# The values' products ahead of queries and keys in two attention layers

## The chip, the cores and the metric

The kernel runs on one core of a Trainium2 chip. The metric is the device time of one execution in microseconds (us). The core has five engines with instruction streams of their own: TensorE (PE, matrix products; PEld is its loading of stationary operands), VectorE (DVE), ScalarE (ACT), GpSimd (POOL) and SyncE (SP, which starts the DMA transfers). They wait for each other through semaphores. TensorE writes to PSUM, a memory of eight banks with 512 float32 values per partition each.

## The reference, cut to what matters

The whole program is a block with two feed-forward parts and an mLSTM mixer on 272 tokens, followed by a second block with two attention layers on 256 tokens and 1024 channels. The change is in the first step of these two layers:

```python
for l in range(DEPTH_2):                                   # two layers
    shift, scale, gate = jnp.split(c_act @ w_ada[l] + b_ada[l], 3, axis=-1)
    h = rms_norm(x, pre_norm_g[l]) * (1.0 + scale[:, None, :]) + shift[:, None, :]
    proj = h @ w_in[l]                                     # 256 x 1024 times 1024 x 4096
    q, k, v = proj[..., 0:A], proj[..., A:2*A], proj[..., 2*A:3*A]   # A = 512 columns each
    ...                                                    # gates and convolution from the rest
    att = dilated_attention(q, k, v, rel_bias) * jax.nn.silu(g_att)
    x = x + gate[:, None, :] * rms_norm(jnp.concatenate([att, cnv], axis=-1) @ w_out[l], post_norm_g[l])
```

## The kernel before

**Products.** Each float32 operand is held as a sum of two float32r parts: the weights as `w1` + `w2`, the layer's input as `u1` + `u2`. A product takes three matmuls: `w1`·`u1`, `w2`·`u1`, `w1`·`u2`. The input is stored with channels on the partitions, in eight tiles (`kt` = 0 to 7) of 128 channels by 256 tokens.

**Weights.** They arrive in chunks of 128 x 1024 values, by one fixed list, in the order of use. SP loads chunk `c` into `raw`, ACT casts it to `w1` (line 738), DVE subtracts to make `w2` (line 1032). There are five slots each. The cast of a chunk waits until TensorE has finished with the chunk five places ahead (`last_of`). The last four casts that ACT makes ahead of a layer are those of the layer's first four chunks; the fifth stands behind the input tiles in ACT's program.

**Boundary into a layer.** Between the previous stage's last product and the layer's first, the kernel normalises. TensorE turns the two scales of the norm into full tiles with transposes (line 373, `spread`): the first, `r1`, goes to PSUM bank 6, the second, `r2`, to bank 5. Then, in steps `k` = 0 to 7, DVE multiplies the previous stage's result by bank 6 (line 1223, `yg`), DVE or POOL adds it to the residual `hT`, DVE multiplies by bank 5 (line 1263, `tmp`), ACT makes `u1` (line 842) and DVE makes `u2` (line 1244). Only the last of the eight readings of a bank raises the bank's semaphore:

```python
m = e.scalar_tensor_tensor(tmp[:, k % 4, 0:n], hT[:, k, OFF[s]:OFF[s] + n], gain(k), ps[:, 5, 0:n],
                           ALU.mult, ALU.mult)
if k == KT - 1:
    m.then_inc(*reading(("r2", s)))
else:
    m.then_inc(*tick(s_tmp, (s, k)))
```

Meanwhile TensorE runs products of a dummy tile `dz` into bank 4 (`dense`, line 329) so that it doesn't stand idle.

**Banks.** `place` gives a block of products its bank: one of banks 0 to 3 in turn, or a bank named by the caller, and it makes TensorE wait until every earlier reading of that bank is done:

```python
if uses[b]:
    e.wait_ge(s_bank[b].handle, uses[b])
```

**The layer before the change.** `head` starts four of the eight query and key blocks together (banks 0 to 3): six `dense` products, then tile by tile eight matmuls with `u1[kt]` (lines 354, 355) and four with `u2[kt]` (line 358). `block` then does one block at a time, 24 matmuls of 256 columns (lines 313 to 315). Behind the eight blocks stand the values: two accumulations of 512 columns in banks 5 and 6, chunk by chunk, 48 matmuls in all (recorded on line 665). Scores (line 629) and twenty more blocks follow. Order on every engine is as the program is written.

Of the kernel before, what the change touches and what calls it, by code (L numbers as in the profile page):

```python
# [13 lines left out]
P = 128  # L14
D = 1024
KT = D // P
S = 256
# [66 lines left out]
def tick(signal, event):  # L84

    signal.count += 1
    signal.at[event] = signal.count
    return signal.handle, 1
# [13 lines left out]
def build(nc, xT, wst, wada, vec, cst, tab, rb, outT):  # L102
    ctx = ExitStack()
    with ctx:
# [184 lines left out]
        def reading(key):  # L289

            return s_bank[bank[key][0]].handle, 1
# [4 lines left out]
        def tensor(e):  # L296
# [20 lines left out]
            def block(key, c, x1, x2, n, mid=None, where=KT - 2):  # L317
                e.wait_ge(s_split.handle, c + 1)
                b = place(key)
                for kt in range(KT):  # L320
                    if mid and kt == where:
                        mid()
                    m = products(ps[:, b, 0:n], c, kt, x1[:, kt, :], x2[:, kt, :], kt == 0, kt == KT - 1)
                m.then_inc(*tick(s_proj, key))
                last_of[c] = key
# [51 lines left out]
            def u_of(s):  # L377
                return (lambda k: (s_u1.handle, at(s_u1, (s, k)))), (lambda k: (s_u2.handle, at(s_u2, (s, k))))
# [240 lines left out]
            def attention(l):  # L619
                x1, x2 = u1[:, :, 0:S], u2[:, :, 0:S]  # L620
                c = C_L[l]

                def scores(k):
                    e.wait_ge(*read(("qk", l, 4 + k)))
                    b_ = [place(("s", l, 2 * k + i), 4 + 3 * i) for i in range(2)]
                    for t in range(2):
                        for i in range(2):
                            hp = 64 * i
                            m = e.matmul(ps[:, b_[i], S * t:S * t + S], qk[l][hp:hp + 64, k, 128 * t:128 * t + 128],  # L629
                                         qk[l][hp:hp + 64, 4 + k, :], start=True, stop=True)  # L630
                    m.then_inc(*tick(s_score, (l, k)))

                def transposes(h):
                    e.wait_ge(s_nrm.handle, at(s_nrm, (l, h, 1)))
                    b = place(("pt", l, h), 5)
                    for j in range(2):
                        for t in range(2):
                            m = e.transpose(ps[:, b, S * j + 128 * t:S * j + 128 * t + 128],  # L638
                                            Sb[l][:, h % 4, t, 128 * j:128 * j + 128], ident)
                    m.then_inc(*tick(s_ptr, (l, h)))  # L640

                def values(k):
                    e.wait_ge(*read(("pt", l, 2 * k + 1)))
                    b = place(("o", l, k), 6)
                    for j in range(2):
                        for i in range(2):
                            h, hp = 2 * k + i, 64 * i
                            m = e.matmul(ps[hp:hp + 64, b, 0:S], Vt[l][:, j, 64 * h:64 * h + 64], PT[l][:, i, j, :],  # L648
                                         start=j == 0, stop=j == 1, skip_group_check=True)
                    m.then_inc(*tick(s_val, (l, k)))  # L650

                keys = [("qk", l, j) for j in range(8)]
                head(keys[:4], c, x1, x2, S, *u_of(f"l{l}"))
                for j in range(4, 8):
                    block(keys[j], c + j, x1, x2, S)
                b_ = [place(("V", l, tt), 5 + tt) for tt in range(2)]
                for c4 in range(4):
                    cc = c + 8 + c4
                    e.wait_ge(s_split.handle, cc + 1)
                    for kk in range(2):  # L660
                        kt = 2 * c4 + kk
                        a, bw = w1[:, cc % NW, 512 * kk:512 * kk + 512], w2[:, cc % NW, 512 * kk:512 * kk + 512]
                        for tt in range(2):
                            for i, (xx, ww) in enumerate(((x1, a), (x1, bw), (x2, a))):
                                m = e.matmul(ps[:, b_[tt], :], xx[:, kt, 128 * tt:128 * tt + 128], ww,  # L665
                                             start=kt == 0 and i == 0, stop=kt == 7 and i == 2)
                    m.then_inc(*tick(s_proj, ("V", l, c4)))
                    last_of[cc] = ("V", l, c4)
                for i in range(21):
                    k, p_ = i // 4, i % 4  # L670
                    if p_ in (0, 1) and 0 < k < 5:
                        transposes(2 * k - 2 + p_)
                    if p_ == 0 and k < 4:
                        scores(k)
                    if p_ == 3 and 0 < k:
                        values(k - 1)
                    if i < 20:
                        block(("g", l, i), c + 12 + i, x1, x2, S)
# [48 lines left out]
        def scalar(e):  # L727
# [12 lines left out]
            def proj(key):  # L740
                e.wait_ge(s_proj.handle, at(s_proj, key))
# [185 lines left out]
            def attention(l):  # L927
                c = C_L[l]

                def tanh_of(key, before):  # L930
                    proj(key)
                    if before:
                        e.wait_ge(*read(before))
                    e.activation(cw_[l][:, 4, :], out_of(key), ACT.Tanh, scale=0.5).then_inc(*tick(s_tanh, key))

                def split_mix(k, src):
                    e.copy(m1[l][:, k, :], src).then_inc(*tick(s_m1, (l, k)))

                split_to(c + NW - 1)
                for j in range(8):  # L940
                    if j > 3:
                        split_to(c + j + NW - 1)
                    proj(("qk", l, j))
                    b = bank_of(("qk", l, j))
                    e.copy(qk[l][:, j, :], ps[:, b, S - 1::-1] if j < 4 else ps[:, b, 0:S]).then_inc(*reading(("qk", l, j)))
                split_to(c + 11 + NW - 1)
                proj(("V", l, 3))
                for tt in range(2):
                    e.copy(Vt[l][:, tt, :], ps[:, 5 + tt, :]).then_inc(*reading(("V", l, tt)))

                def transposes(h):
                    e.wait_ge(s_ptr.handle, at(s_ptr, (l, h)))
                    if h > 1:
                        e.wait_ge(s_val.handle, at(s_val, (l, h // 2 - 1)))
                    e.copy(PT[l][:, h % 2, :, :], ps[:, 5, :].rearrange("p (j q) -> p j q", q=S)).then_inc(
                        *reading(("pt", l, h)))

                def scores(k):
                    for i in range(2):
                        h = 2 * k + i  # L960
                        e.wait_ge(s_max.handle, at(s_max, (l, h)))
                        for t in range(2):
                            e.activation(Sb[l][:, h % 4, t, :], Sb[l][:, h % 4, t, :], ACT.Exp, bias=st_[l][:, h % 4, t:t + 1],
                                         accum_out=st_[l][:, h % 4, 2 + t:3 + t]).then_inc(*tick(s_exp, (l, h, t)))

                before = None
                for i in range(21):
                    k, p_ = i // 4, i % 4
                    if p_ in (0, 1) and 0 < k < 5:
                        transposes(2 * k - 2 + p_)  # L970
                    if p_ == 0 and k < 4:
                        scores(k)
                    if p_ == 3 and 0 < k:
                        e.wait_ge(*read(("o", l, k - 1)))
                        split_mix(k - 1, at_[l][:, (k - 1) % 2, :])
                    if p_ == 0 and k > 1:
                        e.wait_ge(s_cp.handle, at(s_cp, (l, k - 2)))
                        split_mix(4 + k - 2, cw_[l][:, 2, :])
                    if i == 20:
                        break  # L980
                    key = ("g", l, i)
                    split_to(c + 12 + i + NW - 1)
                    if i < 4 or p_ == 3:
                        tanh_of(key, before)
                        before = key
                    elif p_ == 0:
                        proj(key)
                        if k > 1:
                            e.wait_ge(*read(("g", l, i - 3)))
                        e.copy(cw_[l][:, 0, :], out_of(key)).then_inc(*reading(key))  # L990
# [821 lines left out]
```

## Time and profile before

| | before |
|---|---|
| median of 3 runs | 806.5 us (806.33 to 807.24) |
| the profiled execution | 806.2 us, of which 804.2 us is the span of the profile |
| TensorE busy | 795.3 us (99%) |
| VectorE busy | 594.5 us (74%) |
| ScalarE busy | 416.5 us (52%) |
| GpSimd busy | 143.6 us (18%) |
| granted TensorE clock, mean | 0.992 of full speed |

The span is the time from the first to the last recorded instruction, 2.0 us less than the execution's time. Shares of busy time are averages over the span. Matmul records overlap: a record lasts from issue to the last result, so a stream of them is read from the starts. "Granted clock" is 1.00 at 2.4 GHz and 0.50 at 1.2 GHz. The rows that matter are listed further down.

### The profile page before, as it was taken

What the parts mean: (1) busy time and instruction counts of PE and PEld (TensorE: products, weight loads), DVE (VectorE), ACT (ScalarE), POOL (GpSimd) and SP (SyncE); (2) the same over time, 40 slices, a digit from 0 to 9 for tenths busy, and PEclk for the clock granted to TensorE, in tenths of its full rate; (3) what the DMA queues carried; (4) which work ended last, traced back from release to release, by engine and by line L of the source; (5) the groups of instructions that cost most, each with busy time, mean ns of one, the idle gap of its engine ahead of it and who ended that gap; (6) DMA issues with size and microseconds to landing.
All of it is one profiled execution on the core that took longest, in us unless ns stands there. A gap on an engine that the chain in (4) does not pass through costs nothing.

```text
span 804.2 us, 15615 instructions
## 1 busy us (share of the span) xinstructions
PE 795.3 (99%) x6338; PEld 771.1 (96%) x6338; DVE 594.5 (74%) x952; ACT 416.5 (52%) x710; POOL 143.6 (18%) x159
## 2 busy tenths in 40 slices
PE   9999999999999999999999999999999999999997
PEld 9999999999999999999999999999899999999986
DVE  6877777698786976778777779996667568567753
ACT  7444444454367565565444445536555454555541
POOL 3800000041320000020000004230245302035510
PEclk9999999999899999999999999999999999999999
DMA  9876777695436632559867679546544651744531
GB/s 342 308 250 226 233 247 249 204 325 178 122 112 215 192 130 81 182 175 298 287 218 266 241 239 339 177 145 211 163 151 129 185 161 53 264 154 133 157 106 52
DMA packets 45190, 158.83 MB, mean 197 GB/s; under 512 B 5040, under 2 KB 6576, under 8 KB 45120
## 3 DMA queue, kind: packets, MB, share of 16 engines
q1 hardware_dynamic: 45120, 157.85, 59.1%
q8 instruction: 50, 0.82, 0.4%
q14 instruction: 20, 0.16, 0.1%
HBM read 156.76 MB, written 1.06 MB: 196 GB/s over the span
## 4 chain that ended last, share of the span: by engine, by line
PE 97%; issue 1%; DVE 1%; POOL 0%; ACT 0%; DVEq 0%; POOLq 0%
PE ps L313 26%; PE ps L315 25%; PE ps L314 25%; PE ps L665 3%; PE ps L354 2%; PE ps L358 2%; PE ps L355 2%; PE ps L366 2%; PE ps L329 1%; PE ps L557 1%; PE ps L629 1%; PE ps L648 1%; PE ps L638 1%; PE ps L691 1%; PE ps L689 1%
## 5 line engine op out<-in xcount | busy, mean ns | idle before, releaser
L1032 DVE TENSOR_TENSOR w<-raw,w 128x1024 fp32r<-128x1024 f32 x245 | 300.0, 1238 | 132.6 <-ACT w L738 132.2
L313 PE MATMUL ps<-u,w 128*128 128x256 f32 (+1 forms) x1231 | 353.2, 287 | 0.0
L315 PE MATMUL ps<-u,w 128*128 128x256 f32 (+1 forms) x1231 | 349.6, 284 | 0.0
L314 PE MATMUL ps<-u,w 128*128 128x256 f32 (+1 forms) x1231 | 349.0, 284 | 0.0
L738 ACT CAST w<-raw 128x1024 fp32r<-128x1024 f32 x245 | 254.0, 1049 | 122.4 <-PE ps L315 102.7
L313 PEld LDWEIGHTS ps<-u,w 128*128 128x128 f32 x1231 | 232.0, 188 | 6.2 <-issue 4.3
L315 PEld LDWEIGHTS ps<-u,w 128*128 128x128 f32 x1231 | 232.3, 189 | 0.0
L314 PEld LDWEIGHTS ps<-u,w 128*128 128x128 f32 x1231 | 231.7, 188 | 0.0
L313 PE MATMUL ps<-h,w 128*128 128x272 f32 (+1 forms) x352 | 99.7, 283 | 0.0
L314 PE MATMUL ps<-h,w 128*128 128x272 f32 (+1 forms) x352 | 99.3, 282 | 0.0
L315 PE MATMUL ps<-h,w 128*128 128x272 f32 (+1 forms) x352 | 99.1, 282 | 0.0
L1582 POOL TENSOR_TENSOR sqa<-sqa,sq 128x272 f32<-128x272 f32 (+1 forms) x12 | 14.1, 1175 | 311.0 <-ACT sq L803 311.0
L313 PEld LDWEIGHTS ps<-h,w 128*128 128x128 f32 x352 | 66.2, 188 | 0.0
L314 PEld LDWEIGHTS ps<-h,w 128*128 128x128 f32 x352 | 66.1, 188 | 0.0
L315 PEld LDWEIGHTS ps<-h,w 128*128 128x128 f32 x352 | 66.1, 188 | 0.0
L1616 POOL TENSOR_SCALAR Sb<-Sb,st 128x256 f32<-128x256 f32 x32 | 45.2, 1428 | 87.7 <-DVE st L1460 87.7
L1051 DVE SCALAR_TENSOR_TENSOR acc<-adr,cact,acc 128x1024 f32<-128x1024 f32 x42 | 57.3, 1383 | 0.4 <-DMA adr<-wada 0.4
L781 ACT ACTIVATE si<-tmp 128x272 f32<-128x272 f32 (+1 forms) x44 | 18.7, 425 | 70.4 <-DVE tmp L1144 70.4
L1149 DVE TENSOR_TENSOR hf<-si,ps 128x272 f32<-128x272 f32 (+1 forms) x44 | 18.9, 430 | 21.1 <-ACT si L781 21.1
L1593 POOL TENSOR_TENSOR rst<-sst,eps 128x2 f32<-128x2 f32 (+1 forms) x4 | 3.0, 748 | 149.7 <-DVE sst L1195 135.1
L354 PE MATMUL ps<-u,w 128*128 128x256 f32 (+1 forms) x105 | 28.2, 297 | 1.0 <-ACT u L842 0.7
L355 PE MATMUL ps<-u,w 128*128 128x256 f32 (+1 forms) x105 | 27.6, 293 | 0.0
(246 smaller groups left out, 1043.1 us busy)
## 6 DMA issues: line engine op xcount, KB each, us to landing
raw<-wst SPq DMA_DIRECT2D x245, 512.0 KB, 4.6
adr<-wada SPq DMA_DIRECT2D x48, 512.0 KB, 4.0
Bt<-bias_rows SPq DMA_DIRECT2D x8, 192.0 KB, 3.9
hT<-xT SPq DMA_DIRECT2D x4, 272.0 KB, 4.5
outT<-yg SPq DMA_DIRECT2D x4, 256.0 KB, 2.0
cs<-cst SPq DMA_DIRECT2D x1, 140.0 KB, 5.3
cs<-cst SPq DMA_DIRECT2D x1, 128.0 KB, 6.5
vc<-vec SPq DMA_DIRECT2D x1, 101.0 KB, 3.7
```

What stands on the lines that cost most here:

```text
L313: e.matmul(out, a, x1, start=first, stop=False)
L314: e.matmul(out, a, x2, start=False, stop=False)
L315: return e.matmul(out, b, x1, start=False, stop=last)
L354: e.matmul(ps[:, b, 0:n], w1[:, (c + j) % NW, o:o + P], x1[:, kt, :], start=i == 0, stop=False)
L355: e.matmul(ps[:, b, 0:n], w2[:, (c + j) % NW, o:o + P], x1[:, kt, :], start=False, stop=False)
L665: m = e.matmul(ps[:, b_[tt], :], xx[:, kt, 128 * tt:128 * tt + 128], ww, start=kt == 0 and i == 0, stop=kt == 7 and i == 2)
L738: e.copy(w1[:, k % NW, :], raw[:, k % NRAW, :]).then_inc(*tick(s_upper, k))
L781: e.activation(si[f][:, j % 2, :], zg[:, j % 2, 0:n], ACT.Silu).then_inc(*tick(s_si, (f, j)))
L1032: e.tensor_tensor(w2[:, k % NW, :], raw[:, k % NRAW, :], w1[:, k % NW, :].bitcast(F32), ALU.subtract).then_inc(*tick(s_split, k))
L1051: e.scalar_tensor_tensor(a, w, x, a, ALU.mult, ALU.add).then_inc(*tick(s_acc, k))
L1149: e.tensor_tensor(hf[f][:, i, :], si[f][:, i, :], out_of(ku, n), ALU.mult).then_inc(*reading(ku))
L1616: e.tensor_scalar(Sb[l][:, h % 4, t, :], Sb[l][:, h % 4, t, :], st_[l][:, h % 4, 4 + t:5 + t], None, ALU.mult).then_inc(*tick(s_nrm, (l, h ...
```

## The change

In each attention layer TensorE no longer begins with `head`. It places the two accumulations of the values (banks 5 and 6), runs the six `dense` products, and takes the input tile by tile for the values: four matmuls of 512 columns with `u1[kt]`, two with `u2[kt]`. All eight query and key blocks follow with `block`. The weights' chunks are reordered to match, and so is ACT's program. DVE, POOL and SP keep their programs. The number of matmuls and their shapes stay the same.

```diff
-                keys = [("qk", l, j) for j in range(8)]
-                head(keys[:4], c, x1, x2, S, *u_of(f"l{l}"))
-                for j in range(4, 8):
-                    block(keys[j], c + j, x1, x2, S)
-                b_ = [place(("V", l, tt), 5 + tt) for tt in range(2)]
-                for c4 in range(4):
-                    cc = c + 8 + c4
...
+                b_ = [place(("V", l, t), 5 + t) for t in range(2)]
+                high, low = u_of(f"l{l}")
+                dense(6)
+                for kt in range(KT):
+                    cc, o = c + kt // 2, 512 * (kt % 2)
                     e.wait_ge(s_split.handle, cc + 1)
...
+                    a, bw = w1[:, cc % NW, o:o + 512], w2[:, cc % NW, o:o + 512]
+                    e.wait_ge(*high(kt))
+                    for t in range(2):
+                        e.matmul(ps[:, b_[t], :], x1[:, kt, 128 * t:128 * t + 128], a, start=kt == 0, stop=False)
+                        e.matmul(ps[:, b_[t], :], x1[:, kt, 128 * t:128 * t + 128], bw, start=False, stop=False)
+                    e.wait_ge(*low(kt))
+                    for t in range(2):
+                        m = e.matmul(ps[:, b_[t], :], x2[:, kt, 128 * t:128 * t + 128], a, start=False, stop=kt == KT - 1)
+                    if kt % 2:
+                        m.then_inc(*tick(s_proj, ("V", l, kt // 2)))
+                        last_of[cc] = ("V", l, kt // 2)
+                for j in range(8):
+                    block(("qk", l, j), c + 4 + j, x1, x2, S)
...
-                split_to(c + NW - 1)
+                split_to(c + 3 + NW - 1)
+                proj(("V", l, 3))
+                for tt in range(2):
+                    e.copy(Vt[l][:, tt, :], ps[:, 5 + tt, :]).then_inc(*reading(("V", l, tt)))
                 for j in range(8):
-                    if j > 3:
-                        split_to(c + j + NW - 1)
+                    split_to(c + 4 + j + NW - 1)
...
-                split_to(c + 11 + NW - 1)
-                proj(("V", l, 3))
-                for tt in range(2):
-                    e.copy(Vt[l][:, tt, :], ps[:, 5 + tt, :]).then_inc(*reading(("V", l, tt)))
...
+        parts.append(w[:, 1024:1536].reshape(4, 2, P, 512).transpose(0, 2, 1, 3).reshape(4, P, CH))
         parts.append(cols(w[:, 0:1024]))
-        parts.append(w[:, 1024:1536].reshape(4, 2, P, 512).transpose(0, 2, 1, 3).reshape(4, P, CH))
```

TensorE at the boundary into layer 0, before the change, from the fill between the two spreads to the first tile's products (`ps<-cs,rst` is a spread, `ps<-dz` a fill product, `bank5_read` the count of readings of bank 5, `u1_made` that of ready tiles):

```order
L329 MATMUL ps<-dz 128x256 x6
L373 MATMUL ps<-cs,rst 128x128 [waits bank5_read,pow_made]
L373 MATMUL ps<-cs,rst 128x128
L329 MATMUL ps<-dz 128x256 [waits bank2_read,bank1_read,bank3_read,bank0_read,w2_made]
L329 MATMUL ps<-dz 128x256 x5
L354 MATMUL ps<-u,w 128x256 [waits u1_made]
```

The same place with the change:

```order
L329 MATMUL ps<-dz 128x256 x6
L373 MATMUL ps<-cs,rst 128x128 [waits bank5_read,pow_made]
L373 MATMUL ps<-cs,rst 128x128
L329 MATMUL ps<-dz 128x256 [waits bank6_read,bank5_read]
L329 MATMUL ps<-dz 128x256 x5
L661 MATMUL ps<-w,u 128x512 [waits u1_made,w2_made]
L662 MATMUL ps<-w,u 128x512
L661 MATMUL ps<-w,u 128x512
L662 MATMUL ps<-w,u 128x512
L665 MATMUL ps<-w,u 128x512 [waits u2_made]
```

The first fill product behind the second spread waited for readings of banks 0 to 3 and now waits for those of banks 5 and 6; the products behind the fill are of 512 columns.

ACT behind the input tiles of layer 0, before the change (`u<-tmp,mod` is `u1`, `w<-raw` a chunk's cast, `qk<-ps` a block's copy out of PSUM):

```order
L842 ACTIVATE u<-tmp,mod 128x256 [waits tmp_made] x7
L842 ACTIVATE u<-tmp,mod 128x256 [waits bank5_read]
L738 CAST w<-raw 128x1024 [waits proj_done,raw_landed4]
L945 COPY qk<-ps 128x256 [waits proj_done] x4
L738 CAST w<-raw 128x1024 [waits proj_done,raw_landed0]
L738 CAST w<-raw 128x1024 [waits proj_done,raw_landed1]
L738 CAST w<-raw 128x1024 [waits proj_done,raw_landed2]
L738 CAST w<-raw 128x1024 [waits proj_done,raw_landed3]
```

And with the change:

```order
L740 CAST w<-raw 128x1024 [waits proj_done,raw_landed4]
L740 CAST w<-raw 128x1024 [waits proj_done,raw_landed0]
L740 CAST w<-raw 128x1024 [waits proj_done,raw_landed1]
L740 CAST w<-raw 128x1024 [waits proj_done,raw_landed2]
L944 COPY Vt<-ps 128x512 [waits proj_done]
L944 COPY Vt<-ps 128x512
L740 CAST w<-raw 128x1024 [waits proj_done,raw_landed3]
L949 COPY qk<-ps 128x256 [waits proj_done]
```

Four casts stand ahead of the first copy out of PSUM where one stood, and the values' copies come first.

## Rows read from the trace of the kernel before

**Rows 1.** The page: span, busy time of each engine, chain that ended last.

```profile
span 804.2 us, 15615 instructions
PE 795.3 (99%) x6338; PEld 771.1 (96%) x6338; DVE 594.5 (74%) x952; ACT 416.5 (52%) x710; POOL 143.6 (18%) x159
...
PE 97%; issue 1%; DVE 1%; POOL 0%; ACT 0%; DVEq 0%; POOLq 0%
```

**Rows 2.** Timeline of PE, boundary into layer 0: start, length, line, operation, idle before.

```profile
534.25 0.43 PE L373 MATMUL ps<-cs,rst 128*128 128x128 f32 x2 [0.45 <-POOL rst L1598]
534.49 0.95 PE L329 MATMUL ps<-dz 128*128 128x256 f32 x6
535.79 0.39 PE L354 MATMUL ps<-u,w 128*128 128x256 f32 x1 [0.35 <-ACT u L842]
...
537.33 0.28 PE L354 MATMUL ps<-u,w 128*128 128x256 f32 x1
...
538.75 0.28 PE L354 MATMUL ps<-u,w 128*128 128x256 f32 x1
```

**Rows 3.** Timeline of DVE and ACT there: last readings of banks 6 and 5.

```profile
535.45 0.47 DVE L1263 SCALAR_TENSOR_TENSOR tmp<-hT,G,ps 128x256 f32<-128x256 f32 x1
...
542.40 0.41 DVE L1223 TENSOR_TENSOR yg<-yg,ps 128x256 f32<-128x256 f32 x1
...
543.83 0.47 DVE L1263 SCALAR_TENSOR_TENSOR tmp<-hT,G,ps 128x256 f32<-128x256 f32 x1
...
535.96 0.51 ACT L842 ACTIVATE u<-tmp,mod 128x256 fp32r<-128x256 f32 x1 [0.21 <-DVE tmp L1263]
```

**Rows 4.** The same boundary into layer 1, PE and DVE.

```profile
669.56 0.43 PE L373 MATMUL ps<-cs,rst 128*128 128x128 f32 x2 [0.27 <-POOL rst L1598]
671.11 0.39 PE L354 MATMUL ps<-u,w 128*128 128x256 f32 x1 [0.38 <-ACT u L842]
...
679.16 0.47 DVE L1263 SCALAR_TENSOR_TENSOR tmp<-hT,G,ps 128x256 f32<-128x256 f32 x1
```

**Rows 5.** Timeline of PE: sixth query and key block, values, scores (layer 0); values, scores (layer 1).

```profile
550.15 0.39 PE L313 MATMUL ps<-u,w 128*128 128x256 f32 x1
...
558.78 11.29 PE L665 MATMUL ps<-w,u 128*128 128x512 f32 x48
570.00 1.14 PE L629 MATMUL ps<-qk 64*128 64x256 f32 x8
...
694.08 11.29 PE L665 MATMUL ps<-w,u 128*128 128x512 f32 x48
705.30 1.13 PE L629 MATMUL ps<-qk 64*128 64x256 f32 x8
```

**Rows 6.** Timeline of PE, boundary out of the first feed-forward part.

```profile
215.20 0.90 PE L373 MATMUL ps<-cs,rst 128*128 128x128 f32 x3 [0.50 <-POOL rst L1598]
216.03 1.65 PE L329 MATMUL ps<-dz 128*128 128x256 f32 x6
217.48 0.43 PE L354 MATMUL ps<-u,w 128*128 128x272 f32 x1
...
219.52 0.43 PE L354 MATMUL ps<-u,w 128*128 128x272 f32 x1
...
221.52 0.29 PE L354 MATMUL ps<-u,w 128*128 128x272 f32 x1
...
222.66 0.28 PE L354 MATMUL ps<-u,w 128*128 128x272 f32 x1
```

**Rows 7.** Busy time by half microseconds: PE, PEld, DVE, ACT, POOL, granted clock, DMA.

```profile
221.00:221.50 0.50, 0.50 (x4) 0.50 (x3) 0.50 (x3) 0.30 (x1) 0.00 (x0) 0.53 0.00 0
...
340.50:341.00 0.50, 0.50 (x5) 0.38 (x4) 0.38 (x2) 0.00 (x0) 0.46 (x1) 0.93 0.00 0
341.00:341.50 0.50, 0.50 (x4) 0.48 (x3) 0.00 (x0) 0.00 (x0) 0.00 (x0) 0.50 0.00 0
...
344.00:344.50 0.50, 0.50 (x5) 0.50 (x4) 0.50 (x3) 0.00 (x0) 0.28 (x1) 0.65 0.86 352
```

**Rows 8.** Waits of PEld in layer 0, 536 to 666 us: total, times, longest.

```profile
PEld ps L313 <- DVE w L1032: 0.7, 2, 0.4
```

**Rows 9.** The page's costliest groups: casts and subtractions of the chunks.

```profile
L1032 DVE TENSOR_TENSOR w<-raw,w 128x1024 fp32r<-128x1024 f32 x245 | 300.0, 1238 | 132.6 <-ACT w L738 132.2
...
L738 ACT CAST w<-raw 128x1024 fp32r<-128x1024 f32 x245 | 254.0, 1049 | 122.4 <-PE ps L315 102.7
```

More of the change, by code:

```diff
@@ L650, in values @@
                     m.then_inc(*tick(s_val, (l, k)))
-                keys = [("qk", l, j) for j in range(8)]
-                head(keys[:4], c, x1, x2, S, *u_of(f"l{l}"))
-                for j in range(4, 8):
-                    block(keys[j], c + j, x1, x2, S)
-                b_ = [place(("V", l, tt), 5 + tt) for tt in range(2)]
-                for c4 in range(4):
-                    cc = c + 8 + c4
-                    e.wait_ge(s_split.handle, cc + 1)
-                    for kk in range(2):
-                        kt = 2 * c4 + kk
-                        a, bw = w1[:, cc % NW, 512 * kk:512 * kk + 512], w2[:, cc % NW, 512 * kk:512 * kk + 512]
-                        for tt in range(2):
[L664 to L668, printed above, removed]
+                b_ = [place(("V", l, t), 5 + t) for t in range(2)]
[3 more added lines that the diff above has]
+                    cc, o = c + kt // 2, 512 * (kt % 2)
+                    e.wait_ge(s_split.handle, cc + 1)
+                    a, bw = w1[:, cc % NW, o:o + 512], w2[:, cc % NW, o:o + 512]
[11 more added lines that the diff above has]
+                    block(("qk", l, j), c + 4 + j, x1, x2, S)
                 for i in range(21):
@@ L946, in attention @@
                 split_to(c + 11 + NW - 1)
-                proj(("V", l, 3))
-                for tt in range(2):
-                    e.copy(Vt[l][:, tt, :], ps[:, 5 + tt, :]).then_inc(*reading(("V", l, tt)))
                 def transposes(h):
```

## The prediction

> **What bounds the kernel now.** I first read the page's busy times and chain: TensorE is busy for 795.3 of 804.2 us and makes up 97% of the chain that ended last [rows 1]. So a microsecond in which TensorE stands still is a microsecond of the result, and nothing that only relieves VectorE or ScalarE shows. Then I read TensorE's timeline at the boundary into layer 0, the place where the new order begins. The second spread starts at 534.25, six fill products at 534.49, and the first tile's products of the four query and key blocks at 535.79, after 0.35 us of idle time that ended with the first `u1` tile [rows 2]. The head's steps then start at 537.33 and 538.75 [rows 2], 1.42 us each; eight of them keep TensorE busy while VectorE is still normalising. That cover is what the change must keep. Third I read who uses banks 5 and 6 in that time. VectorE reads bank 6 for the last time from 542.40 to 542.81, and bank 5 from 543.83 to 544.30 [rows 3]. Fourth, for the price of a stop, I looked at the two other boundaries of the kernel, where the granted clock is at half [rows 6, 7].
>
> **The change, part by part.** *The new wait.* The values' accumulations are placed in banks 5 and 6, and these hold the two scales from which VectorE is making the very input tiles that the values' products want. Only the eighth reading raises a bank's semaphore. The first fill product behind the second spread now waits for both banks, and TensorE works in order, so behind it stand the other five fill products, all products of values, queries and keys, and everything later. Bank 5 comes last. VectorE's normalisation waits for nothing of TensorE's behind the second spread, so it runs as before and reaches its last reading at 544.30. A consumer starts about 0.05 us after such a step: a `tmp` ends at 535.92 and ScalarE takes it at 535.96 [rows 3]. So the fill starts at 544.35 instead of 534.49. TensorE's last work ahead of it, the spread, ends at 534.68 [rows 2], which leaves 9.67 us without an instruction. All of it lay under TensorE's work before: the head covered it.
>
> *The fill.* Six fill products take 1.45 us from their first start to the next instruction's where the clock is at half (216.03 to 217.48 [rows 6]). At full clock the last of six ends 0.95 us after the first start [rows 2]; a record of 0.28 us leaves 0.67 for five steps, 0.13 each, so a next instruction would start after about 0.8 us. What the clock is after this stop I take from the nearest rows: at the boundary out of the first feed-forward part 0.50 us of idle time ahead of 215.20 among short instructions went with products at half speed [rows 6], and at the one out of the mixer the clock fell to 0.50 without any stop, at about 340.93 (a mean of 0.93 over the half microsecond puts 0.07 us of it at half) [rows 7]. A stop of 9.67 us, almost twenty times the longest of these, can hardly leave it at full. I take 1.45, and the values start at 544.35 + 1.45 = 545.80. Their place in the sequence was 535.79: a shift of 10.0 us (9.35 at full clock, 544.35 + 0.79 - 535.79). Layer 1 repeats it: the last reading of bank 5 ends at 679.63, the values start at 679.68 + 1.45 = 681.13, and the head started at 671.11 [rows 4]: 10.0 us.
>
> *The rest of the half clock.* No 512-column product at half clock is in the trace. The nearest rows are the 272-column products of the first boundary: nine of them take 2.04 us (217.48 to 219.52) at half and 1.14 us (221.52 to 222.66) at full clock [rows 6], 0.227 and 0.127 us each. In proportion to the columns a values' product takes 0.427 us at half clock; at full clock 48 take 11.22 us (558.78 to 570.00), 0.234 us each [rows 5]. So a stretch at half clock loses 1 - 0.234/0.427 = 45% of itself. How long it lasts behind the resumption has two bounds: from 215.20 to the return at about 221.47 (a mean of 0.53) it is 6.25 us, from 340.93 to the return at about 344.35 it is 3.4 us (0.65 as the mean of the last half microsecond) [rows 6, 7]. Less the 1.45 us of fill already counted, 1.95 to 4.8 us lose 0.9 to 2.2 us; I take the middle, 1.5, since the two rows are equally near. The Trainium skill (TensorE: Matmul & The Clock Gate, What's actually happening) says that an idle TensorE drops to 1.2 GHz and has to be busy for a while before it gets 2.4 GHz back, which speaks against this change in the same way. The same page (Wait — 56ns, not 53.3ns?) gives 426.7 and 215.7 ns between 512-column products at the two clocks; by these the stretch would lose 49% and my middle would be 1.7 instead of 1.5 us. The trace's 234 ns at full clock is above the page's 215.7, and no row here shows the 426.7.
>
> *The moved products.* Before, the head and four blocks took 558.78 - 535.79 = 22.99 us. Now eight blocks stand there. Three took 558.78 - 550.15 = 8.63 us [rows 5], 2.88 each, so eight take 23.0. The values' 48 products are the same in either place (11.22 us in both layers [rows 5]). By the time that they start, all input tiles are made or within 1 us of it, so their tile-by-tile waits find nothing to wait for. I cost this at 0.
>
> *The weights.* The values need chunks `c` to `c+3`, which are cast ahead of the normalisation as the head's four were. The next cast, of `c+4`, stands behind the tiles on ScalarE as before and is long done when the first query block wants it, now some 21 us later. Slots then come free one every 2.8 us instead of four together, and a cast (1.05 us) and a subtraction (1.24 us) per slot fit in [rows 9]. Before, weights that VectorE had not yet made cost TensorE 0.7 us in a layer [rows 8]. That is the most this part can give; part of it was hidden under queued products, so I take 0 and keep -0.7 for the range. SP's program is the same list of loads with other addresses; it is ahead by five chunks at the stop and so gains nothing that TensorE could use. ScalarE's two copies of the values (banks 5 and 6 again) move from behind the last chunk of values to before the query blocks; the next user of either bank comes twelve blocks behind the values.
>
> *Sum.* A layer: 10.0 + 1.5 + 0 + 0 = 11.5 us. Two layers: 23.0. On the profiled execution's 806.2 us (804.2 span, 2.0 around it) that is 829.2 us; the median of the runs shown, 806.5, is 0.3 above that execution, and I add that. I predict 829.5.
>
> **The rivals.** *The stop without the clock.* The wait is as above but the clock is at full when work resumes: 9.35 a layer, 18.7 together, 824.9 us. For it speaks only that the boundaries into the two layers are the ones that kept full clock so far, with fill products in between; against it that those fills are what now waits. 4%.
>
> *The stop is partly given back.* The same stop, but ready weights and tiles behind it save TensorE's little waits: 0.7 us a layer, so 1.4 off whatever else holds, 827.9 us with the clock's price. Against it: TensorE is the bound in the whole rest of the program, and the other engines can run no more than five chunks ahead. 8%.
>
> *No stop at all, the other side.* The values start with the first tile. That needs bank 5 free of its last reading by about 535.2, when the fill would be over, and not at 544.30. Then a tile's step is six products of 0.234, 1.40 us, against 1.42 in the head, 0.2 us less in eight steps, and with the 0.7 us of weights' waits gone the layer would win 0.9, the kernel 1.8: 804.4 us. The point from which it decides is a wait of 0.9 us: if the last reading came later than that behind the fill, the change loses. Such a start would mean that the wait in the order shown is met by an earlier reading than the eighth; the program's count of readings gives bank 5 one reading for the whole scale, the eighth, which speaks against it. 3%, with a case in which stop and gain cancel within noise inside it at 1%.
>
> **How the numbers follow.** The likeliest, stop and half clock without giving back, has 85%, and its own range is that of the half clock: 806.2 + 2 x (10.0 + 0.9) = 828.0 to 806.2 + 2 x (10.0 + 2.2) = 830.6. To hold eight in ten with the unknown parts, the range reaches down towards the stop without the clock (824.9) and up to 831.5, since a stop much longer than any in the trace may keep the clock at half somewhat longer than 6.25 us. What this kernel's measurement can tell from no change is about 0.2%, 1.6 us. All cases with the stop are slower by over 2%: 97%. Faster has 2%, within 0.2% has 1%.
>
> **What would show it.** Right: in the changed kernel's timeline TensorE has one idle stretch of about 9.7 us in front of the first fill product at each of the two boundaries, released by VectorE's `tmp` step; granted clock 0.50 from there until 2 to 5 us into the values' products; the values' records longer there; TensorE's busy share falls from 99 to about 97%; no other group of waits grows. The eight blocks behind take 23.0 us. Wrong: if the idle stretch is released by anything else, if it is shorter than 9 us, or if the clock stays at 1.00, the size is off; if the first product of values starts within a microsecond of the first `u1` tile, the whole argument is.

## The result and the profile after

The changed kernel takes 827.77 us (median of 4 runs, 826.95 to 828.75); the kernel before took 806.55 us in 4 runs beside it. The ratio is 1.026 with a 95% interval of 1.0247 to 1.0273: slower by 21.2 us. The profiled execution took 828.75 us, with a span of 826.8, so it is 22.55 us above the profiled execution of before and a microsecond above its own median. Its terms are read against the profile of before, the comparison of kernels against the medians.

The page of the changed kernel: span, busy times, and the chain that ended last by engine; these answer to [rows 1].

```profile
span 826.8 us, 15633 instructions
PE 799.4 (97%) x6338; PEld 774.6 (94%) x6338; DVE 595.5 (72%) x952; ACT 416.5 (50%) x710; POOL 144.0 (17%) x159
...
PE 94%; DVE 4%; issue 1%; ACT 0%; POOL 0%; DVEq 0%; POOLq 0%
```

TensorE's busy time grew by 4.1 us with the same 6338 matmuls, and VectorE has 4% of the chain where it had 1%. The waits of TensorE in the changed kernel, total, times, longest, say where:

```profile
PE ps L329 <- DVE tmp L1264: 19.2, 2, 9.6
```

The timeline of TensorE at the boundary into layer 0, answering to [rows 2], and into layer 1, answering to [rows 4]: start, length, line, operation, idle before.

```profile
533.95 0.43 PE L373 MATMUL ps<-cs,rst 128*128 128x128 f32 x2 [0.47 <-POOL rst L1599]
544.00 1.65 PE L329 MATMUL ps<-dz 128*128 128x256 f32 x6 [9.62 <-DVE tmp L1264]
545.45 0.63 PE L661 MATMUL ps<-w,u 128*128 128x512 f32 x1
545.87 0.63 PE L662 MATMUL ps<-w,u 128*128 128x512 f32 x1
...
557.94 0.28 PE L313 MATMUL ps<-u,w 128*128 128x256 f32 x1
...
580.72 1.13 PE L629 MATMUL ps<-qk 64*128 64x256 f32 x8
...
681.07 0.63 PE L373 MATMUL ps<-cs,rst 128*128 128x128 f32 x2
691.30 1.65 PE L329 MATMUL ps<-dz 128*128 128x256 f32 x6 [9.61 <-DVE tmp L1264]
692.75 0.63 PE L661 MATMUL ps<-w,u 128*128 128x512 f32 x1
...
705.04 0.28 PE L313 MATMUL ps<-u,w 128*128 128x256 f32 x1
...
727.82 1.14 PE L629 MATMUL ps<-qk 64*128 64x256 f32 x8
```

VectorE's timeline there, answering to [rows 3]: the last reading of bank 5.

```profile
543.47 0.47 DVE L1264 SCALAR_TENSOR_TENSOR tmp<-hT,G,ps 128x256 f32<-128x256 f32 x1
```

It ends at 543.94 and the fill starts at 544.00 ("the resumption" from here on: the first product behind the stop). By then all input tiles but the last `u1` and the last two `u2` are made; the values' products come when nothing is left to cover. A useful measure of a layer is the time from the start of the second spread to the start of the scores, since everything that moved lies between them: before, 35.75 us (534.25 to 570.00) and 35.74 (669.56 to 705.30) [rows 2, 4, 5]; now 46.77 and 46.75. That is 22.0 of the 22.6 us by which the span grew. The rest lies between the layers: from the first scores to layer 1's second spread it is 99.56 us before and 100.35 now, less 0.3 us by which layer 0's second spread came earlier. The clock was at half there from 678.2 to 681.6 in this execution. The profiles of the kernels below have 99.5 to 99.6 us in the same place where the clock stayed at full, and 100.05 and 100.06 us in the two others where it was at half, so the order isn't the cause.

Busy time and granted clock (the number behind the five engines) of the changed kernel, early and late in the stop and where full speed came back in layer 0, then early in the stop and where full speed came back in layer 1:

```profile
534.50:536.00 1.50, 0.00 (x0) 0.00 (x0) 1.50 (x4) 0.85 (x2) 1.23 (x2) 0.62 0.04 14
...
540.00:544.00 4.00, 0.01 (x1) 0.01 (x1) 4.00 (x10) 1.55 (x4) 1.88 (x3) 0.50 0.00 0
...
548.00:548.50 0.50, 0.50 (x3) 0.40 (x2) 0.00 (x0) 0.00 (x0) 0.00 (x0) 0.50 0.44 172
548.50:549.00 0.50, 0.50 (x4) 0.42 (x3) 0.00 (x0) 0.00 (x0) 0.00 (x0) 0.99 0.87 336
...
684.00:686.00 2.00, 0.00 (x0) 0.00 (x0) 1.97 (x5) 0.51 (x1) 0.72 (x1) 0.76 0.00 0
...
695.00:695.50 0.50, 0.50 (x3) 0.41 (x2) 0.00 (x0) 0.00 (x0) 0.00 (x0) 0.72 1.25 156
```

Full speed is back 4.5 us after the resumption in layer 0 (544.00 to 548.50) and about 4.0 us after it in layer 1 (691.30 to 695.28, from the mean of 0.72). It had fallen at about 534.9 in layer 0, 0.5 us after TensorE's last work (534.38), and only at about 685.0 in layer 1, 3.4 us after it (681.69).

### The profile page after: what moved, and what is told of

Read it like the earlier page. It is cut to its first block, busy times and chain, and to the rows that moved or that the text cites. A ratio compares the mean times of both kernels' runs of the same rounds, so it can differ in the third digit from the quotient of the medians.

```text
span 826.8 us, 15633 instructions
## 1 busy us (share of the span) xinstructions
PE 799.4 (97%) x6338; PEld 774.6 (94%) x6338; DVE 595.5 (72%) x952; ACT 416.5 (50%) x710; POOL 144.0 (17%) x159
## 4 chain that ended last, share of the span: by engine, by line
PE 94%; DVE 4%; issue 1%; ACT 0%; POOL 0%; DVEq 0%; POOLq 0%
PE ps L313 26%; PE ps L315 25%; PE ps L314 25%; PE ps L366 2%; PE ps L329 2%; DVE tmp L1264 1%; PE ps L358 1%; PE ps L557 1%; PE ps L354 1%; PE ps L355 1%; PE ps L629 1%; PE ps L661 1%; PE ps L662 1%; PE ps L665 1%; PE ps L648 1%
## 5 line engine op out<-in xcount | busy, mean ns | idle before, releaser
L313 PEld LDWEIGHTS ps<-u,w 128*128 128x128 f32 x1287 | 242.6, 189 | 6.2 <-issue 4.3
L315 PEld LDWEIGHTS ps<-u,w 128*128 128x128 f32 x1287 | 242.9, 189 | 0.0
L314 PEld LDWEIGHTS ps<-u,w 128*128 128x128 f32 x1287 | 242.2, 188 | 0.1
L329 PE MATMUL ps<-dz 128*128 128x256 f32 x86 | 19.3, 373 | 20.4 <-DVE tmp L1264 19.2
L329 PEld LDWEIGHTS ps<-dz 128*128 128x128 f32 x86 | 16.3, 269 | 21.1 <-DVE tmp L1264 19.9
```

The costliest lines, as they stand in the source:

```text
L313: e.matmul(out, a, x1, start=first, stop=False)
L314: e.matmul(out, a, x2, start=False, stop=False)
L315: return e.matmul(out, b, x1, start=False, stop=last)
L329: e.matmul(ps[:, 4, 0:256], dz[:, 0:128], dz[:, :], start=True, stop=True)
```

## The experiments

The theory: the whole loss is the wait for the last reading of banks 5 and 6, with the half clock that follows it; the order of values and queries counts for nothing. The rivals: the order itself costs; the clock costs nothing net; the two layers' losses are not independent. Each kernel was also profiled once; the table gives, from these profiles, the time from the second spread to the scores in both layers, as defined above. The ratios are to runs of the kernel before on the same chip: 806.55 us for the changed kernel, 806.31 for the first four experiments, 806.27 (7 runs, 805.02 to 808.00) for the last three. The profiled execution need not be a typical one: for five of the kernels (changed, bank 6, no fill behind, 40 fill products, layer 0 only) it is the slowest of four.

| kernel | median us (runs, lowest to highest) | ratio to before, 95% interval | profiled execution, us | layer 0, layer 1 |
|---|---|---|---|---|
| before | 806.31 (15, 805.42 to 807.34) | 1 | 806.2 | 35.75, 35.74 |
| changed | 827.77 (4, 826.95 to 828.75) | 1.026 (1.0247 to 1.0273) | 828.75 | 46.77, 46.75 |
| values in free banks | 806.39 (11, 805.62 to 810.34) | 1.0005 (0.9995 to 1.0016) | 806.24 | 36.21, 35.82 |
| one accumulation in bank 6 | 826.06 (4, 825.11 to 827.71) | 1.0243 (1.0229 to 1.0257) | 827.71 | 45.77, 46.29 |
| 80 fill products ahead of the wait | 823.82 (4, 823.49 to 827.82) | 1.0224 (1.0204 to 1.0244) | 823.67 | 44.82, 44.85 |
| the wait alone, old order | 828.24 (4, 827.10 to 829.54) | 1.0268 (1.0254 to 1.0282) | 827.10 | 46.39, 46.55 |
| no fill behind the wait | 827.81 (4, 827.48 to 829.43) | 1.0271 (1.0251 to 1.029) | 829.43 | 46.29, 46.74 |
| 40 fill products ahead | 829.28 (4, 828.24 to 829.45) | 1.0282 (1.0264 to 1.03) | 829.45 | 47.09, 47.04 |
| stop in layer 0 only | 818.09 (4, 816.45 to 818.20) | 1.0139 (1.0117 to 1.0162) | 818.20 | 47.64, 35.90 |

**The new order without the wait.**

```diff
-                b_ = [place(("V", l, t), 5 + t) for t in range(2)]
+                b_ = [place(("V", l, t)) for t in range(2)]
...
-                    e.copy(Vt[l][:, tt, :], ps[:, 5 + tt, :]).then_inc(*reading(("V", l, tt)))
+                    e.copy(Vt[l][:, tt, :], ps[:, bank_of(("V", l, tt)), :]).then_inc(*reading(("V", l, tt)))
```

> The changed order, but the values' accumulations in the next two of banks 0 to 3 in place of banks 5 and 6. Theory (the wait for the last reading of banks 5 and 6 is the whole loss): no idle stretch in front of the fill, the first product of values within 0.1 us of the first u1 tile, and a time of 806.5 us, between 804.4 and 807.0. Rival (the order itself costs, because 512-column products with tile-by-tile waits are paced by VectorE, or because later work moves): 810 us or more with no 9.6 us stop. Rival (the loss is split): 815 to 820 us.

Measured: 806.39 us against 806.31, no difference (the interval reaches from 0.4 us faster to 1.3 us slower). The timeline of TensorE at the boundary into layer 0 in this kernel:

```profile
533.72 0.69 PE L373 MATMUL ps<-cs,rst 128*128 128x128 f32 x2 [0.29 <-POOL rst L1599]
534.06 1.63 PE L329 MATMUL ps<-dz 128*128 128x256 f32 x6
535.62 0.77 PE L661 MATMUL ps<-w,u 128*128 128x512 f32 x1
...
537.43 0.39 PE L661 MATMUL ps<-w,u 128*128 128x512 f32 x1
...
538.82 0.39 PE L661 MATMUL ps<-w,u 128*128 128x512 f32 x1
```

The values start with the first tile, and a tile's step is 1.39 us (537.43 to 538.82), as short as the head's 1.42. So tile by tile the values cover the normalisation as well as four query and key blocks do, once they have banks of their own. The order is neither a cost nor a gain that these runs can tell. The 36.21 us of layer 0, 0.46 above the kernel before, go with the clock, which was at half here without any stop, from about 533.0 to 536.4 (the fill took 1.56 us):

```profile
536.00:536.50 0.50, 0.50 (x2) 0.37 (x2) 0.50 (x2) 0.20 (x1) 0.07 (x1) 0.64 0.00 0
```

**The wait without the new order.** The kernel before, with one line more ahead of `head`:

```diff
+                e.wait_ge(s_bank[5].handle, uses[5])
                 head(keys[:4], c, x1, x2, S, *u_of(f"l{l}"))
```

> The kernel before the change, with its own order, and one wait more: TensorE waits for the last reading of bank 5 ahead of the head in both layers. Theory (the wait is all, the order counts for nothing): the time of the changed kernel, 827.8 us, within 1 us. Rival (the new order costs or gains something beside the wait): off by more than 1.5 us, lower if the order costs, higher if it gains.

Measured: 828.24 us, 0.5 above the changed kernel, with intervals that overlap widely. Together these two runs show both halves: the order alone costs 0.1 us, the wait alone 21.9. The timeline of TensorE in this kernel shows the same stop, ended by the same step, in front of the old head:

```profile
543.97 1.65 PE L329 MATMUL ps<-dz 128*128 128x256 f32 x6 [9.62 <-DVE tmp L1264]
545.42 0.41 PE L354 MATMUL ps<-u,w 128*128 128x256 f32 x1
```

**Another reading to wait for.** One accumulation in one of banks 0 to 3, the other in bank 6 (the copy out as in the first experiment):

```diff
-                b_ = [place(("V", l, t), 5 + t) for t in range(2)]
+                b_ = [place(("V", l, 0)), place(("V", l, 1), 6)]
```

> The changed kernel, but only one of the two accumulations stands in a bank that VectorE reads in the normalisation: bank 6, whose last reading (line 1224 of the changed kernel) ends at 542.47 in its trace, 1.47 us ahead of bank 5's at 543.94; the other has one of banks 0 to 3. Theory: the stop ends with the yg step of k = 7 and is 8.1 us instead of 9.6, so 2 x 1.47 = 2.9 us less than 827.8: 824.9 us. Rival (any one wait on a later bank costs the same, or the stop is set by the input tiles): 827.8 us. Rival (bank 5 was all): 806 us.

Measured: 826.06 us, 1.7 below the changed kernel; 2.9 was expected. The expected 824.9 would be a ratio of 1.0231, just inside the interval, and the rival's 827.8 would be 1.0267, outside it; but the interval overlaps that of the changed kernel, so it is the trace that decides. The waits of TensorE in this kernel:

```profile
PE ps L329 <- DVE yg L1224: 16.5, 2, 8.2
```

The stop is now ended by the multiplication with bank 6, and the two are 2.8 us shorter together (8.23 us each, against 9.62 and 9.61), close to the 2.9 that the readings are apart. The layers are only 1.5 us shorter together in these profiles. What is missing lies behind the stop: the values' products took 12.85 and 13.23 us here (544.82 to 557.67, 690.78 to 704.01) against 12.49 and 12.29 in the changed kernel, 1.3 us more. The windows of this kernel show full speed coming back at about 548.57, 5.2 us after the resumption at 543.40:

```profile
548.50:549.00 0.50, 0.50 (x3) 0.39 (x3) 0.00 (x0) 0.00 (x0) 0.00 (x0) 0.93 1.12 147
```

In layer 1 it came 6.0 us after the resumption (689.36 to 695.35). In the changed kernel it was 4.5 and 4.0 us, so part of what the shorter stop won was lost again to a longer stretch at half speed.

**The stop without the clock.** `dense(80)` ahead of the place of the values:

```diff
+                dense(80)
                 b_ = [place(("V", l, t), 5 + t) for t in range(2)]
```

> The changed kernel with 80 more fill products between the second spread and the wait for banks 5 and 6, in both layers: 80 x 0.1175 = 9.4 us of work where TensorE stood still, so the stop stays and only the clock differs. Theory (of 11.0 us that a layer loses, 9.3 are the stop and 1.8 the half clock: 0.66 in the six fill products behind, 1.17 in the values' products): 2 x 1.8 = 3.6 us less, 824.1 us, granted clock 1.00 throughout. Rival (the clock costs nothing net, since something else paces the values): 827.8 us.

Measured: 823.82 us, 4.0 below the changed kernel, where 3.6 was expected; the two intervals don't overlap, though one of the four runs took 827.82. TensorE's timeline and the windows in this kernel:

```profile
533.75 10.92 PE L329 MATMUL ps<-dz 128*128 128x256 f32 x86
544.51 0.40 PE L662 MATMUL ps<-w,u 128*128 128x512 f32 x1
```

```profile
534.00:544.50 10.50, 10.39 (x86) 10.19 (x86) 10.24 (x23) 4.40 (x9) 4.37 (x6) 1.00 0.02 5
544.50:549.00 4.50, 4.50 (x22) 3.67 (x21) 1.96 (x5) 1.67 (x2) 0.00 (x0) 1.00 0.37 97
```

TensorE is busy all through and its clock stays at full, yet the values start no sooner than VectorE lets them: its last reading of bank 5 ends at 543.64 here, and the values follow 0.87 us later, at 544.51, behind the last six fill products. The profile shows no idle stretch of TensorE here, and the kernel is still 17.5 us slower than before: the useful work waits behind useless work. A layer loses 9.1 us here (44.82 and 44.85 against 35.75) and 11.0 with the clock, so the clock is 1.9 of it, as in the changed kernel's own rows (0.66 in the fill and 1.27 in the values' products).

**Half of the stop covered.** `dense(40)` in place of `dense(80)`.

> The changed kernel with 40 fill products ahead of the wait, 40 x 0.1175 = 4.7 us, so that a stop of about 4.9 us is left of 9.6. Theory (the resumption is set by VectorE, and a stop of this length costs the clock as the longer one does): 827.8 us, no gain from covering half of it. Rival (a shorter stop leaves the clock at full): 824 us, as with 80 fill products.

Measured: 829.28 us, where 827.8 was expected (a ratio of 1.0267, inside the interval). It is 1.5 us above the changed kernel, with intervals that overlap; covering half the stop gains nothing. The windows of this kernel around the stop, which lasts from 539.56 to 544.41:

```profile
540.00:542.00 2.00, 0.00 (x0) 0.00 (x0) 2.00 (x6) 0.61 (x2) 1.17 (x2) 1.00 0.00 0
542.00:544.00 2.00, 0.00 (x0) 0.00 (x0) 2.00 (x5) 0.91 (x2) 0.99 (x2) 0.69 0.00 0
544.00:546.00 2.00, 1.59 (x7) 1.59 (x8) 1.52 (x6) 1.44 (x2) 0.00 (x0) 0.50 0.00 0
```

The clock is still at full in the first microseconds without work, but falls before the stop ends, at about 542.75, and comes back 5.2 us after the resumption. The price is then no smaller than that of the long stop.

**The fill ahead of the wait in place of behind it.**

```diff
+                dense(6)
                 b_ = [place(("V", l, t), 5 + t) for t in range(2)]
                 high, low = u_of(f"l{l}")
-                dense(6)
```

> The changed kernel with its six fill products ahead of the wait for banks 5 and 6 in place of behind it. Theory (behind a stop the fill is no cover but 1.45 us of work at half clock, which the values' products must wait for): the values start 1.45 us sooner after the stop; since the half clock then lies on more of them, some 0.45 x 1.45 = 0.65 us of that is lost again, 0.8 us less a layer, 826.2 us. Rival (without the fill the clock comes back so much later that nothing is left): 827.8 us or more.

Measured: 827.81 us and a ratio of 1.0271 (1.0251 to 1.029). The expected 826.2 would be 1.0247, outside the interval: this expectation failed, and its rival held. The values do start at once (TensorE's timeline in this kernel):

```profile
546.00 0.79 PE L661 MATMUL ps<-w,u 128*128 128x512 f32 x1 [8.90 <-DVE tmp L1264]
```

but full speed comes back later. Its windows in layer 0 and in layer 1:

```profile
550.50:551.00 0.50, 0.50 (x3) 0.40 (x2) 0.00 (x0) 0.00 (x0) 0.00 (x0) 0.56 0.77 270
...
697.50:698.00 0.50, 0.50 (x3) 0.40 (x2) 0.00 (x0) 0.50 (x1) 0.00 (x0) 0.79 0.00 0
```

That is 4.9 us after the resumption at 546.00 and 5.9 us after that at 691.84, against 4.5 and 4.0 in the changed kernel. My estimate had taken the length of the stretch at half speed as given. Whether the missing fill products caused the later return or chance did, one profile each cannot say, and it stays open; other kernels here, with the fill in place, had returns as late (5.9 and 6.0 us).

**One layer only.** `place(("V", l, t), 5 + t if l == 0 else None)`, with the copy out as in the first experiment.

> The changed kernel, but in layer 1 the values' accumulations stand in two of banks 0 to 3; layer 0 keeps banks 5 and 6. Theory (each layer's wait costs its 10.7 us by itself and nothing is given back later): half of the loss, 806.4 + 10.7 = 817.1 us. Rival (the second stop is partly paid by the first, or the reverse): off by more than 1.5 us.

Measured: 818.09 us against the expected 817.1: 1.0 us off, less than the 1.5 that the rival asks for. Layer 1 is back at 35.90 us, layer 0 has its stop. Its 47.64 us is the longest of all the profiles, with a resumption at 544.52 and half speed until 550.40, 5.9 us (from the mean of 0.60 in its windows). The clock was at half before the stop began, from about 533.3 (the mean of 0.83), so the second spread at 534.22 already ran slow, with a record of 0.69 us:

```profile
533.00:533.50 0.50, 0.50 (x6) 0.50 (x5) 0.47 (x3) 0.00 (x0) 0.03 (x1) 0.83 0.84 295
...
550.00:550.50 0.50, 0.50 (x3) 0.40 (x2) 0.00 (x0) 0.00 (x0) 0.00 (x0) 0.60 0.33 131
```

The losses of the two layers add up, and nothing of the first is given back later: of the 12.0 us by which this profiled execution exceeds that of before, 11.9 are in layer 0.

## Why the prediction was right

The forecast was 829.5 us with a range of 825.0 to 831.5; the median is 827.77. It lies 0.2 us below the range of the likeliest case (828.0 to 830.6), whose mechanism is the one that occurred.

*The new wait.* Right in place, cause and size: two idle stretches of 9.62 and 9.61 us (predicted 9.67) in front of the first fill product, released by `tmp`. VectorE ran as before: its last reading ended 9.99 us after the start of the second spread, 10.05 in the kernel before. One other wait reads longer, 0.78 us in front of the products at 343.40, where it was 0.23; it lies ahead of both layers, and the kernels with free banks, with 80 fill products and with the wait alone have it too.

*The fill.* Six products took 1.45 us at half clock in both layers, as taken from [rows 6]. From second spread to first product of values it is 11.50 us (533.95 to 545.45) where the head started after 1.54: a shift of 9.96 us, predicted 10.0. Layer 1: 11.68 after 1.55, 10.13 us; its second spread already ran at half clock there, and its record is 0.2 us longer.

*The half clock behind the fill.* Right in kind, too large in size. The values' 48 products took 12.49 us (545.45 to 557.94) and 12.29 us (692.75 to 705.04) in place of 11.22, so it cost 1.27 and 1.07 us, where I took 1.5 and bounds of 0.9 and 2.2. I had put 3.4 and 6.25 us as bounds on the time from resumption to full clock; in this execution it was 4.5 and 4.0. That the size came out within its bounds is in part luck. Neither row measured what follows a stop: at the mixer's boundary there was none, and at the other the clock fell at about 214.64, while TensorE's last product ahead of the 0.50 us of idle time was still running (it ended at 214.70). The kernel before, busy time and granted clock:

```profile
214.50:215.00 0.50, 0.20 (x2) 0.00 (x0) 0.47 (x3) 0.00 (x0) 0.50 (x1) 0.64 0.00 0
```

And the experiments had returns after 2.9 us, below my lower bound, as well as after 6.0. A values' product at half clock takes 0.427 us (545.45, 545.87, 546.30), the price that I had scaled from 272-column products. The Trainium skill's 426.7 ns (TensorE: Matmul & The Clock Gate, Wait — 56ns, not 53.3ns?) agrees with it.

*The moved products.* I put the exchange of head and four blocks for eight blocks at 0. It gave back 0.2 us a layer: 22.78 us (557.94 to 580.72, and 705.04 to 727.82) against 22.99 and 22.97.

*The sum.* 9.96 + 1.27 - 0.21 = 11.02 us and 10.13 + 1.07 - 0.19 = 11.01 us a layer, predicted 11.5. The profiled execution comes to 828.75 where the sum gave 829.2. That is closer than the terms were: the two layers were put 1.0 us too high, and the 0.5 us by which the time outside them grew, with the clock between the layers, was in no term. The median is 1 us below this profile, and the clock differs from execution to execution in the same sense: the granted mean was 0.978 in the profiled one (828.75 us) and 0.979, 0.982 and 0.982 in the others (828.05, 827.50 and 826.95).

*The weights.* My allowance of -0.7 us a layer rested on a row for the stretch from 536 to 666 us [rows 8], and that was too wide a window. In the kernel before it lies whole in 570 to 666 us, behind the start of the scores. In the changed kernel the same 0.7 us is still there, and narrowed to 581 to 667 us, behind the scores' start, it is whole. The waits of PEld in that stretch:

```profile
PEld ps L313 <- DVE w L1033: 0.7, 2, 0.4
```

There was nothing to give back where the order changed. The experiment with free banks shows it: with the stop gone, nothing is won.

*The rivals.* The stop without the clock was put at 824.9 us; made to order with 80 fill products it is 823.8. A start without a stop was put at 804.4 us if it had occurred; made with free banks it is 806.4. Its two gains were a shorter step and the weights' waits: the first, 0.2 us in eight steps, doesn't show (layer 1 took 35.82 us there against 35.74), the second was in another place. The rival of a stop that is partly given back was put at 827.9 us, nearer to the median than my 829.5, but what it rests on did not happen: the weights' waits stayed, and behind the stop 0.2 us a layer came back where it had 0.7. My forecast lay above the median for other reasons: the half clock behind the fill cost less than I took, and the median lies 1 us below the profile that the terms were read from.

## What to carry to other kernels

When work is moved ahead, look not only at its inputs but at its outputs' buffers: a PSUM bank that is free at the old place may be in use at the new one, and here it held the very scales from which the inputs were being made. Waiting per tile for inputs is worth nothing if the destination is released only once, after the last tile. A loss of this kind is found by reading what released the idle stretch (a reader of the bank, not a maker of the input), and undone by another bank; filling the stop with dummy products wins back the clock, 1.9 of 11.0 us here, and makes the profile look busy without bringing the work forward.

## What the runs showed of the hardware

The return to full clock after a stop is scattered. With the same stop of 9.6 us and the same six fill products behind it, it came 4.5 and 4.0 us after the resumption in the changed kernel and 5.9 us after it in the kernel with one stop. In the one with the wait alone it came after 4.0 us in layer 1 (689.66 to 693.63) and after 2.9 us in layer 0: resumption at 543.97, and in its windows

```profile
546.50:547.00 0.50, 0.50 (x4) 0.50 (x4) 0.15 (x1) 0.00 (x0) 0.00 (x0) 0.64 0.00 0
```

so at about 546.86. Each microsecond of that costs 0.45 us, so a stop has a spread of its own of about 1.4 us, of the size of the effects that three of these experiments looked for (1.5, 1.8 and 0.8 us a layer).

The fall of the clock is scattered as well. With 40 fill products ahead it was at 1.00 for some 3 us without any instruction, and at half before 4.85 us were over; in the changed kernel it fell 0.5 us into the stop of layer 0 and 3.4 us into that of layer 1. In three of the profiles (free banks, the wait alone, stop in layer 0 only) it fell at about 533 us, among the short products ahead of the second spread and before there was any long stop. So every stop in these profiles (4.6 to 9.6 us) went with half clock, but half clock did not always come from a stop.
